# Differential attention: both probability maps weighted on VectorE, before the rotary pieces

## The reference, cut to what matters

```python
def diff_attend(q, k, v, lam):
    s = jnp.einsum('bqhmd,bthmd->bhmqt', q * ATTN_SCALE, k).astype(jnp.float32)
    p = jax.nn.softmax(s, axis=-1)
    w = (p[:, :, 0] - lam * p[:, :, 1]).astype(v.dtype)
    return jnp.einsum('bhqt,bthe->bqhe', w, v)
```

## Time and profile before

| what | value |
|---|---|
| median of 3 runs | 2686.13 us (2683.16 to 2688.63) |
| the profiled execution: its time, its span | 2685.78 us, 2684.0 us |
| mean granted TensorE clock in it | 0.969 |
| busy: PE, DVE, ACT, POOL | 2456.2, 1176.4, 1154.6, 988.8 us |
| differential heads, layer 0 / layer 1 | about 318 to 571 us / 1842 to 2042 us of the span |

### The profile page before, as it was taken

How to read it: one execution, slowest core, us unless ns; L and a number is a source line. 1 busy time by engine, 2 the same in 40 slices (tenths; PEclk the granted TensorE clock), 3 DMA queues, 4 the chain that set the end, 5 groups by cost and what they waited for, 6 DMA issues and landing times.

```text
span 2684.0 us, 34267 instructions
## 1 busy us (share of the span) xinstructions
PE 2456.2 (92%) x13556; PEld 2189.7 (82%) x13556; DVE 1176.4 (44%) x1802; ACT 1154.6 (43%) x2266; POOL 988.8 (37%) x771
## 2 busy tenths in 40 slices
PE   5989899979998898999999998889988979899998
PEld 2878888869987897999999996777776767688887
DVE  3566555569973322111111125666557983311111
ACT  4565666653244425322321335566674234432221
POOL 0211112147456533544543542112222545444443
PEclk8999999989998998999999998999998999999999
DMA  5100111113233422332332322101111224233332
GB/s 207 55 24 25 32 32 32 40 59 106 67 92 119 154 63 79 110 95 79 110 110 70 110 81 79 40 25 48 40 37 54 75 71 134 79 102 94 96 96 91
DMA packets 62077, 209.02 MB, mean 78 GB/s; under 512 B 7392, under 2 KB 7648, under 8 KB 61664
## 3 DMA queue, kind: packets, MB, share of 16 engines
q1 hardware_dynamic: 61920, 206.84, 24.4%
HBM read 202.62 MB, written 4.19 MB: 77 GB/s over the span
## 4 chain that ended last, share of the span: by engine, by line
PE 46%; DVE 10%; ACT 5%; issue 1%; ACTq 0%; DVEq 0%
PE acc L522 14%; PE acc L524 14%; PE acc L523 14%; DVE X L1494 5%; ACT M L892 2%; PE sco L616 2%; DVE M L1387 2%; DVE RB L1387 1%; ACT H L892 1%; ACT WHI L888 1%; PE aux L679 1%; PE sco L666 1%; DVE NM L1430 1%; ACT RB L892 0%; PE aux L522 0%
## 5 line engine op out<-in xcount | busy, mean ns | idle before, releaser
L446 POOL TENSOR_TENSOR WLO<-STG,WHI 128x512 fp32r<-128x512 f32 (+2 forms) x760 | 984.7, 1322 | 1671.8 <-ACT WHI L888 1671.7
L522 PE MATMUL acc<-H,WHI 128*128 128x384 f32 (+2 forms) x2048 | 747.0, 365 | 44.8 <-DVE H L1387 29.1
L523 PE MATMUL acc<-H,WHI 128*128 128x384 f32 (+2 forms) x2048 | 725.7, 354 | 0.0
L524 PE MATMUL acc<-H,WLO 128*128 128x384 f32 (+2 forms) x2048 | 724.8, 354 | 0.0
L888 ACT ACTIVATE WHI<-STG 128x512 fp32r<-128x512 f32 (+2 forms) x760 | 407.8, 590 | 539.7 <-PE acc L524 419.5
L522 PEld LDWEIGHTS acc<-H,WHI 128*128 128x128 f32 x2048 | 390.8, 191 | 92.0 <-issue 26.1
L524 PEld LDWEIGHTS acc<-H,WLO 128*128 128x128 f32 x2048 | 390.9, 191 | 26.9
L523 PEld LDWEIGHTS acc<-H,WHI 128*128 128x128 f32 x2048 | 392.0, 191 | 23.8
L522 PE MATMUL acc<-RB,WHI 128*128 128x384 f32 (+1 forms) x816 | 294.0, 360 | 30.7 <-issue 20.7
L1494 DVE SCALAR_TENSOR_TENSOR X<-U,WDW,X 128x783 f32<-128x783 f32 (+1 forms) x248 | 290.3, 1171 | 17.3 <-ACT X L892 9.7
L523 PE MATMUL acc<-RB,WHI 128*128 128x384 f32 (+1 forms) x816 | 291.1, 357 | 0.0
(11 more groups left out here) (123 smaller groups left out, 2896.9 us busy)
## 6 DMA issues: line engine op xcount, KB each, us to landing
STG<-in_w_fi SPq DMA_DIRECT2D x88, 512.0 KB, 3.5
STG<-in_w_mod SPq DMA_DIRECT2D x80, 512.0 KB, 3.5
STG<-in_w_in SPq DMA_DIRECT2D x52, 512.0 KB, 3.5
STG<-in_w_gate SPq DMA_DIRECT2D x48, 512.0 KB, 3.5
STG<-in_w_fo SPq DMA_DIRECT2D x32, 512.0 KB, 3.5
STG<-in_w_br SPq DMA_DIRECT2D x48, 256.0 KB, 2.6
FIRST<-in_w_mod SPq DMA_DIRECT2D x8, 1024.0 KB, 18.8
STG<-in_w_out SPq DMA_DIRECT2D x16, 512.0 KB, 3.6
```

What stands on the lines that cost most here:

```text
L446: nc.gpsimd.tensor_tensor(WLO[:, s, a:a + w], STG[:, g, a:a + w], WHI[:, s, a:a + w].bitcast(F32), ALU.subtract).then_inc(S("w_split"), 1)
L522: nc.tensor.matmul(dst, lh, rh, start=first, stop=False)
L523: nc.tensor.matmul(dst, lh, rl, start=False, stop=False)
L524: return nc.tensor.matmul(dst, ll, rh, start=False, stop=last)
```

## The change

ACT's `weighted` is gone. DVE makes the whole weight of a differential item in one function, `diff_probs`: it waits for the first exponential, takes its reciprocal and scales map 0 by it; then it waits for the second exponential, takes its reciprocal, multiplies it by minus lambda into RLN, and adds map 1 times RLN to map 0. The function is called where `diff_factors` was called, in front of the first slot's pieces. Sums, buffers and the order on PE stay as they were.

```diff
-            def weighted(g, k0):
-
-                slot = 2 * (g % 2) + 1
-                n = TOK if k0 == 0 else CTX
-                c.step("rl")
-                act.wait_ge(S("rl"), c.at("rl"))
-                fn(PR[:, slot, 0:n], PR[:, slot, 0:n], ACT.Copy, scale=RLN[:, g % 2:g % 2 + 1], sem="pb")
-
@@
                     if after:
                         exp(0, g + 1, after[3])
                         exp(1, g + 1, after[3])
-                        if after[0] >= 4:
-                            weighted(g + 1, after[3])
                     slot(j + 1, 2 * i)
@@
-            def diff_factors(l, g):
-                s = 2 * (g % 2)
-                dve.wait_ge(S("exp"), c.at("sc1"))
-                own("recip", nc.vector.reciprocal(RL[:, s:s + 2], L[:, s:s + 2]))
-                tt(RLN[:, g % 2:g % 2 + 1], RL[:, s + 1:s + 2], NEGLAM[:, l:l + 1], ALU.mult).then_inc(S("rl"), 1)
-
-            def diff_probs(g, k0):
+            def diff_probs(l, g, k0):
                 s = 2 * (g % 2)
                 n = TOK if k0 == 0 else CTX
-                c.step("pb")
-                dve.wait_ge(S("pb"), c.at("pb"))
-                nc.vector.scalar_tensor_tensor(PR[:, s, 0:n], PR[:, s, 0:n], RL[:, s:s + 1], PR[:, s + 1, 0:n],
+                dve.wait_ge(S("exp0"), c.at("sc0"))
+                own("recip", nc.vector.reciprocal(RL[:, s:s + 1], L[:, s:s + 1]))
+                nc.vector.tensor_scalar(PR[:, s, 0:n], PR[:, s, 0:n], RL[:, s:s + 1], None, ALU.mult).then_inc(S("pa"), 1)
+                c.step("pa")
+                dve.wait_ge(S("exp"), c.at("sc1"))
+                own("recip", nc.vector.reciprocal(RL[:, s + 1:s + 2], L[:, s + 1:s + 2]))
+                own("rl", tt(RLN[:, g % 2:g % 2 + 1], RL[:, s + 1:s + 2], NEGLAM[:, l:l + 1], ALU.mult))
+                dve.wait_ge(S("pa"), c.at("pa"))
+                nc.vector.scalar_tensor_tensor(PR[:, s, 0:n], PR[:, s + 1, 0:n], RLN[:, g % 2:g % 2 + 1], PR[:, s, 0:n],
                                                ALU.mult, ALU.add).then_inc(S("pn"), 1)
@@
                     if after and after[0] < 4:
                         gqa_probs(g + 1, after[3])
                     elif after:
-                        diff_factors(l, g + 1)
+                        diff_probs(l, g + 1, after[3])
                     slot(j + 1, 2 * i)
-                    if after and after[0] >= 4:
-                        diff_probs(g + 1, after[3])
```

## The result

| | before | changed |
|---|---|---|
| median (range) | 2687.4 us (2683.2 to 2690.1), 4 runs | 2662.45 us (2660.3 to 2663.5), 4 runs |
| ratio | | 0.9908, 95% interval 0.989 to 0.9925 |
| profiled execution, span | 2685.8 us, 2684.0 us | 2662.4 us, 2660.6 us |

A forecast was written before the change was run, and what follows sets the result against it. TensorE, busy 92% of the span, was taken as the bound. From 2685.8 us profiled, chains took 14.1 and clock 6.6, and the median's 0.3 was added: 2665.4 us, own range 2660 to 2670, wider range 2657 to 2677.

The forecast's parts named there:

- The chain of one item: Layer 0, head 5, item 1: exponentials' end to finished weights falls from 2.38 to 1.42 us, scaling hidden; 0.96 us saved.
- A: Layer 0, four heads, items 0 and 1: two waits share one saving, anchored at ScalarE's gate-tile evacuation; 3.8 us.
- B: Layer 0, item 3 of four heads: weights no longer stand behind the normalising of k; 3.8 us.
- C: Layer 0, head 7, item 5: the 256-column scaling leaves ScalarE's queue, which a sub-norm waits for; 0.8 us.
- F: Layer 1, head 7, without rotary pieces: items 1 and 3 wait for the weights alone; 2.1 us.
- D: Layer 1, heads 4 to 6, items 1 and 2: VectorE's chain begins 1.2 us earlier per head; 3.6 us.
- E: Layer 1, heads 4 to 6, item 3: 0.85 us weight wait becomes a longer wait for the scores; gain 0.
- The clock: Five places with low granted clock behind long waits, 8.4 us; four of five taken back, 6.6 us.
- 1: Rival: chain shorter, but clock still falls after layer 0's four waits, or falls elsewhere; 2672.0 us, chance 0.20.
- 2: Rival: a second releaser right behind the first in items with rotary pieces, no clock returns; 2679.4 us, chance 0.10.
- 3: Rival: weight in front makes rotary pieces late at nine first slots in layer 1; slower, 2692 us, chance 0.04.
- 4: Rival: the change does its work and more low-clock stretches vanish; 2655 to 2660 us, chance 0.06.

The follow-up runs named there:

- Experiment 4: Changed kernel with map 0's reciprocal and scaling held back until the second exponential has ended: 2683.9 us, ratio 0.9993.
- experiment 6: Changed kernel with the gate's sigmoid replaced by a copy of the same width, so without two table loads: 2651.7 us, ratio 0.9874.
- Experiment 5: Changed kernel; for item 3's weights in layer 1, heads 4 to 6, scaling before the first slot's rotary pieces, the rest behind: 2658.1 us, again 2656.2 us.
- experiment 1: The changed kernel run again with no edit: 2663.3 us, ratio 0.9921.
- experiment 3: Kernel before, ScalarE still scaling map 0, with the last weight operation moved in front of the first slot's rotary pieces: 2700.8 us, ratio 1.0047.

## Why the prediction was right, point by point

- **The chain of one item.** Forecast 1.42 us from the second reciprocal on and 0.96 saved; measured 1.41 and 0.97. The scaling of the grouped-query items was the right row: none of the 40 took over 0.622 us. Experiment 4 shows that the overlap carries three quarters of it.
- **A, B, C, F** came within 0.2 us of their sizes. A's reasoning (two waits share one saving, anchored at the gate tile) is shown by experiment 6; F's did not see that head 7 in layer 1 has that anchor too.
- **D** measured 4.0 for 3.6 (1.1, 1.4 and 1.5 us in heads 4 to 6, for 1.2 each); item 2's wait stayed at 0.91 to 1.41 us and its items start earlier, as said. The 1.26 us at item 1 was head 4's alone; heads 5 and 6 waited 0.86 and 0.83 us. The sum did not use it.
- **E** was the one place where the order works against the change: nothing forecast, 0.4 measured over the three heads. Of 0.85 and 0.97 us of waiting in head 5 were left 0.40 us in the transposes and 1.24 at the scores, not 1.8 at the scores. I had the low half of k at the same moment as before; it begins 2.95 us behind the start of the second exponential, where it was 3.11. Experiment 5 took most of the rest out.
- **The clock** was the weak term: 6.6 us forecast, 4.2 in the table, and for a wrong reason. I took the wait's length as what decides, with a border between 1.78 and 2.12 us. Thirteen profiles with four places each (item 1 of layer 0's heads, windows as in experiment 1) say: after waits of 2.28 us or more low clock followed 14 times of 19, after 1.81 to 1.84 us 7 of 21, after less than 1.5 us 0 of 12. Elsewhere in the differential heads shorter waits had low clock behind them too: 1.57 us at item 3 of head 7 in experiment 4, and the 1.24 us of the scores in layer 1, head 4, of the changed kernel, which is the new fall of the table. So 1.2 us was no safe side. In the first profile of the changed kernel two of layer 0's four falls are gone, not four, and head 7's in layer 1; those three give 4.6 of the 5.7 us (1.5 each). The other 1.1 us are not the clock's: in heads 4 and 5, which have the same low clock in both traces, the way from item 1 to item 2 is 0.31 and 0.41 us shorter all the same. With the new fall the clock gave 3.1 us. "Four of five" should have been a share: each fall that grows rarer is worth 1.5 us times how much rarer.
- **Rivals.** 1 (the clock stays) was half true in that one trace and not in the second. 2 held only at E, as priced there. 3 did not occur (by its own numbers 1.2 us per place use up what A, B, C and F give together, not only the gain of these heads); experiment 3 shows what it would take, a wait of VectorE in front of the pieces. 4 was reached only with further edits.
- **The 4.1 us elsewhere** had no term in the sum. Two profiles of one program differ by 5 us between the layers, with the clock, so no cause in the change is claimed. The medians differ by 22 to 25 us; chains and clock give 15.1 and 4.2. That the sum came within 3 us of the measured time is in part luck: these 4.1 us stand where the clock's were missing.

## What to carry to other kernels

Price a move of work by the chain it shortens and look for an interval in which a neighbour computes anyway: 0.62 us of scaling placed beside an exponential was, with the reciprocal in front of it, worth 21 us, low clock included; placed behind it, the change as a whole was worth nothing measurable. Then follow the chain back to its anchor before looking further at its end: a 1.15 us copy that could wait, standing in ScalarE's queue two steps ahead, was worth some 7 us, and the order of the weights some 3.5. And before anything is made earlier, look at what it will then stand beside; a pause can be what keeps two engines apart.

## What the runs showed of the hardware

- VectorE operations on SBUF that meet GpSimd's split are stretched by up to about 1.1 us (a split takes 1.3), with two inputs (0.69 to 1.82 us for 512 columns, 1.03 to 2.14 for a pair, 0.16 to 1.06 for one column) and also with one (0.35 to 1.32 us for 256 columns). Not all are: with one operand in PSUM a pair kept its 1.02 us, and the shuffle of `rope` took 0.76 us beside a split (1902.11 in the changed kernel) and 0.73 without.
- A reciprocal of 768 columns on VectorE: 4.95 us, an addition of the same size 0.56.
- TensorE's granted clock behind the same 1.83 us wait was 0.66 in some places and executions and 1.00 in others; low clock was more frequent behind longer waits, and each fall cost 1.5 us. What decides it the runs leave open.
- Two executions of one program, place by place: distances between items agree to 0.03 us within a head and to 0.07 us from one head to the next where the clock is the same; the stretch between the two layers' differential heads differed by 5 us, with TensorE 6.5 us longer busy on the same matmuls.
